# Down-products of the experts as seven quarter products, their weight sums on GpSimd, and half-row scatters

## The reference, cut to what matters

```python
def expert_choice_ffn(h, w_router, w1, w3, w2):
    n_tok, d = h.shape[1], h.shape[2]
    cap = EC_FACTOR * n_tok // N_EXPERTS
    aff = jax.nn.softmax(jnp.einsum('bnd,de->bne', h, w_router).astype(jnp.float32), axis=-1)
    gate, idx = lax.top_k(jnp.swapaxes(aff, 1, 2), cap)
    xs = jax.vmap(lambda hb, ib: hb[ib])(h, idx)
    a = jnp.einsum('becd,edf->becf', xs, w1)
    b = jnp.einsum('becd,edf->becf', xs, w3)
    y = jnp.einsum('becf,efd->becd', jax.nn.silu(a) * b, w2) * gate[..., None].astype(h.dtype)

    def combine(yb, ib):
        return jnp.zeros((n_tok, d), h.dtype).at[ib.reshape(-1)].add(yb.reshape(-1, d))

    return jax.vmap(combine)(y, idx)
...
        x_lat = x_lat + m_lat[5] * expert_choice_ffn(h_lat, router_w[layer], ...)
        if need_ctx:
            x_ctx = x_ctx + m_ctx[5] * expert_choice_ffn(h_ctx, router_w[layer], ...)
```

## Time and profile before

| | us |
|---|---|
| median of three runs | 4462.08 (4459.23 to 4466.95) |
| profiled execution, its own time | 4467.19 |
| its span, first to last instruction | 4465.3 |
| mean granted TensorE clock | 0.965 of full |

### The profile page before, as it was taken

One profiled execution on the slowest core, in us unless ns is written; L12 is line 12 of the kernel. 1 busy time (PEld: TensorE's weight loads), 2 busy tenths in 40 slices (PEclk: granted clock), 3 DMA queues, 4 the chain that ended last, 5 costly groups with the idle time before them and its releaser, 6 DMA issues. The chain is left out here.

```text
span 4465.3 us, 68193 instructions
## 1 busy us (share of the span) xinstructions
PE 4116.9 (92%) x27024; PEld 2569.5 (58%) x27024; DVE 2364.5 (53%) x4884; ACT 1132.7 (25%) x2569; POOL 229.9 (5%) x281
## 2 busy tenths in 40 slices
PE   7996899999999999996999999989999995999997
PEld 4443755888667788664444444458757773333332
DVE  6408334433576544746555555534435646666664
ACT  2011222212575322822200001031135532000001
POOL 0000000000121000000001000000000000000000
PEclk8998999999999999997999999999999996999998
DMA  7658221122421212116667767641161114888986
GB/s 280 250 90 341 70 86 39 65 106 95 156 101 67 74 58 99 33 49 254 244 251 268 280 261 281 266 155 35 51 214 32 21 58 166 322 340 327 344 332 224
DMA packets 133590, 757.35 MB, mean 170 GB/s; under 512 B 14336, under 2 KB 52992, under 8 KB 97904
## 3 DMA queue, kind: packets, MB, share of 16 engines
q1 hardware_dynamic: 108048, 670.05, 40.0%
q0 software_dynamic: 20272, 64.76, 5.4%
q10 hardware_dynamic: 5040, 19.37, 1.2%
HBM read 663.46 MB, written 91.19 MB: 169 GB/s over the span
## 5 line engine op out<-in xcount | busy, mean ns | idle before, releaser
L440 PE MATMUL psum<-w_ring,arena 128*128 128x256 f32 (+1 forms) x2784 | 611.1, 378 | 19.6 <-PEq L199 8.5
L440 PEld LDWEIGHTS psum<-w_ring,arena 128*128 128x128 f32 x2784 | 522.9, 192 | 91.3 <-issue 21.1
L3358 PE MATMUL psum<-arena 128*64 128x512 f32 x2048 | 452.5, 593 | 2.6
L3388 PE MATMUL psum<-arena 128*128 128x512 f32 x1024 | 447.9, 595 | 3.6 <-DVE arena L3655 0.9
L440 PE MATMUL psum<-arena,w_ring 128*128 128x256 f32 x1600 | 354.6, 381 | 6.4 <-DVE arena L495 3.5
L3358 PE MATMUL psum<-w_ring,arena 128*64 128x512 f32 x1536 | 343.8, 597 | 2.8 <-issue 2.8
L440 PEld LDWEIGHTS psum<-arena,w_ring 128*128 128x128 f32 x1600 | 302.9, 191 | 50.1 <-DVE w_ring L536 3.6
L3388 PEld LDWEIGHTS psum<-arena 128*128 128x128 f32 x1024 | 191.9, 190 | 237.4 <-issue 231.2
L3358 PEld LDWEIGHTS psum<-arena 128*64 128x64 f32 x2048 | 151.2, 137 | 272.7 <-issue 270.6
L3506 ACT ACTIVATE arena<-psum 128x512 f32<-128x512 f32 x128 | 76.6, 598 | 911.9 <-PE psum L3358 911.9
L1851 PE MATMUL psum<-arena 48*128 48x512 f32 (+5 forms) x1440 | 291.0, 514 | 8.9 <-PEq L1464 3.5
(11 more groups left out here) (429 smaller groups left out, 5397.8 us busy)
## 6 DMA issues: line engine op xcount, KB each, us to landing
w_ring<-in_wstream SPq DMA_DIRECT2D x162, 2048.0 KB, 9.5
arena<-in_wstream SPq DMA_DIRECT2D x97, 2048.0 KB, 7.8
x_rows<-arena SPq DMA_DIRECT2D x26, 512.0 KB, 2.7
w_ring<-in_wstream ACTq DMA_DIRECT2D x6, 2048.0 KB, 7.7
arena<-x_rows SPq DMA_DIRECT2D x18, 512.0 KB, 7.3
xn_rows<-arena POOLq DMA_DIRECT2D x18, 512.0 KB, 7.2
arena<-f_rows SPq DMA_DIRECT2D x8, 1024.0 KB, 7.3
arena<-x_rows SPq DMA_DIRECT2D x8, 1024.0 KB, 9.4
```

The source lines that it names most:

```text
L440: last = self.cr.nc.tensor.matmul(out, l, r, start=(start and k == 0), stop=(k == len(pairs) - 1), skip_group_check=True)
L3358: last = nc.tensor.matmul(cr.bank[bank][HT * h:HT * (h + 1), :], left[:, k], right[:, 4 * h + k, :], start=(start and k == 0), stop=(k == ...
L3388: last = nc.tensor.matmul(cr.bank[YB[h]][:, :], hid[:, k], W[4 + h][:, k, :], start=(k == 4), stop=(k == 3))
```

## The change

The down-product of each expert, in both layers, is made by the same scheme as the up-products. `hid` is four blocks (r, c), w2 is four blocks: D11 and D21 are tile 4, D12 and D22 tile 5. The host lays w2 out so that a tile holds both a left and a right 256-column piece of each half of the contraction (`lay_out`).

- TensorE: `down(e)` is seven `quarter`s, M1, M2, M6, M5, M7, M3, M4, each 8 matmuls of 64 output rows by 256 columns (L3447 of the new code). The two column halves of a result land on partitions 0 to 63 and 64 to 127 of one bank. In layer 0 `ctx_hidden` stands before `product_7` and `ctx_down` behind it.
- GpSimd: four sums of 128x2048 per expert, V1 = D12 - D11, V2 = D22 - V1, V3 (in D12's place) = D22 - D12, V4 = D21 - V2. V1 has a buffer of its own, V2 and V4 use T1's. V2 waits for `sum_4`, V1 for tiles 4 and 5. In layer 0 V3 waits for `ctx_down`.
- VectorE: `hidden_sums` (four of 256 elements), `out_sums` (four additions from PSUM), `out_top` and `out_bottom`; `sum_1` now also waits for the whole down-product before it (`dn`).
- ScalarE: `keep_y`, three copies out of the down-product's bank.
- The scatter is two indirect DMAs, one for each token half: `yr[r]` is [128, 512], a token's left half row on partition t, its right half on 64 + t, and the row index is doubled (`ix2`). The scatter of expert e - 1 is issued in expert e's turn, before its V sums. At the entry of each layer eight small matmuls and two VectorE instructions make the doubled lists; VectorE waits for them before `sum_0(0)` (layer 1) and `place(0)`.
- SyncE: tile 4 is free after M2, V1 and V4, tile 5 after M3, V2 and V3; its loop is unrolled. The up-products count in one semaphore (`up`) instead of seven.

```diff
+    D11, D21, D12, D22 = W[4][:, 0:4], W[4][:, 4:8], W[5][:, 0:4], W[5][:, 4:8]
+    V2, V4 = T1[:, 0:4], T1[:, 4:8]
...
+    M1B, M2B, M5B, M3B = YB[0], YB[1], HB[0], HB[1]
+    P1, P2, P6, P5, P3, P7, P4 = range(1, 8)
+    M1, M2, M6, M5, M7, M3, M4 = range(1, 8)
+    V_1, V_2, V_4, V_3 = (1, 2, 3, 4) if ctx else (1, 3, 4, 2)
...
+                if j >= 4 and ctx:
+                    sp.wait_ge(k_r, e + 1)
+                if j == 4:
+                    sp.wait_ge(dn, 7 * e + M2)
+                    sp.wait_ge(w2s, 4 * e + V_1)
+                    sp.wait_ge(w2s, 4 * e + V_4)
+                if j == 5:
+                    sp.wait_ge(dn, 7 * e + M3)
+                    sp.wait_ge(w2s, 4 * e + V_2)
+                    sp.wait_ge(w2s, 4 * e + V_3)
...
+            def sum_w1(e):
+
+                loaded(pool, 4, e)
+                loaded(pool, 5, e)
+                if e:
+                    pool.wait_ge(dn, 7 * (e - 1) + M5)
+                elif ctx:
+                    pool.wait_ge(cx_r, 4)
+                nc.gpsimd.tensor_tensor(V1, D12, D11, ALU.subtract).then_inc(w2s, 1)
+
+            def sum_w3(e):
+
+                pool.wait_ge(w2s, 4 * e + V_1)
+                if ctx:
+                    pool.wait_ge(k_r, e + 1)
+                nc.gpsimd.tensor_tensor(D12, D22, D12, ALU.subtract).then_inc(w2s, 1)
+
+            def sums_w2_w4(e):
+
+                pool.wait_ge(t_4, e + 1)
+                pool.wait_ge(w2s, 4 * e + V_1)
+                nc.gpsimd.tensor_tensor(V2, D22, V1, ALU.subtract).then_inc(w2s, 1)
+                pool.wait_ge(w2s, 4 * e + V_2)
+                nc.gpsimd.tensor_tensor(V4, D21, V2, ALU.subtract).then_inc(w2s, 1)
+
+            def scatter(e):
+
+                if e == 0:
+                    pool.wait_ge(dup_ok, 4)
+                for r in range(2):
+                    pool.wait_ge(c_e, 2 * e + r + 1)
+                    if e and r == 0:
+                        pool.wait_ge(sc, SC * e)
+                    pool.indirect_dma_start(out=x_h[:, :], out_offset=bass.IndirectOffsetOnAxis(ap=ix2[:, NE * r + e:NE * r + e + 1], axis=0),
+                                            in_=yr[r].rearrange("p c n -> p (c n)"), in_offset=None, compute_op=ALU.add).then_inc(sc, 16)
+
...
-                pool.wait_ge(c_e, 2 * e + 2)
                 if e:
-                    pool.wait_ge(sc, SC * e)
-                pool.indirect_dma_start(out=x_d[:, :], out_offset=bass.IndirectOffsetOnAxis(ap=ix[:, e:e + 1], axis=0),
-                                        in_=yr, in_offset=None, compute_op=ALU.add).then_inc(sc, 16)
+                    scatter(e - 1)
+                sum_w1(e)
                 if ctx:
-                    pool.wait_ge(k_e, e + 1)
-                    pool.indirect_dma_start(out=x_q[:, :], out_offset=bass.IndirectOffsetOnAxis(ap=ixs[:, e:e + 1], axis=0),
-                                            in_=yc, in_offset=None, compute_op=ALU.add).then_inc(sc, 16)
+                    sums_w2_w4(e)
+                    sum_w3(e)
+                    scatter_ctx(e)
+                else:
+                    sum_w3(e)
+                    sums_w2_w4(e)
+            scatter(NE - 1)
...
-                if ctx and g == 0 and some(e):
-                    pe.wait_ge(k_e, e)
+                if g == 0 and some(e):
+                    pe.wait_ge(c_e, 2 * e)
...
-                    pe.wait_ge(ug_ok, e + 1)
+                    pe.wait_ge(k_e, e + 1)
...
+            def quarter(bank, left, right, start):
+
+                for k in range(4):
+                    for h in range(2):
+                        last = nc.tensor.matmul(cr.bank[bank][HT * h:HT * (h + 1), 0:QW], left[:, k], right[:, k, QW * h:QW * (h + 1)],
+                                                start=(start and k == 0), stop=(k == 3), skip_group_check=True)
+                last.then_inc(dn, 1)
+
+            def down(e):
+
+                loaded(pe, 4, e)
                 if some(e):
-                    pe.wait_ge(c_e, 2 * e + (h - 1))
-                if h == 0:
-                    pe.wait_ge(h_ok, 4 * e + 3)
-                if ctx:
-                    pe.wait_ge(v_ok, e + 1)
-                for k in (4, 5, 6, 7, 0, 1, 2, 3):
-                    if h == 0 and k == 0:
-                        pe.wait_ge(h_ok, 4 * e + 4)
-                    last = nc.tensor.matmul(cr.bank[YB[h]][:, :], hid[:, k], W[4 + h][:, k, :], start=(k == 4), stop=(k == 3))
-                last.then_inc(c_r, 1)
+                    pe.wait_ge(c_e, 2 * e)
+                pe.wait_ge(h_ok, 4 * e + 1)
+                quarter(M1B, h_block(0, 0), D11, True)
+                pe.wait_ge(h_ok, 4 * e + 2)
+                quarter(M2B, h_block(0, 1), D21, True)
+                pe.wait_ge(hs, 4 * e + 3)
+                pe.wait_ge(w2s, 4 * e + V_2)
+                pe.wait_ge(yk, 3 * e + 1)
+                quarter(M1B, HS[1], V2, False)
+                pe.wait_ge(w2s, 4 * e + V_1)
+                quarter(M5B, HS[0], V1, True)
+                pe.wait_ge(w2s, 4 * e + V_3)
+                pe.wait_ge(yk, 3 * e + 2)
+                quarter(M1B, HS[2], D12, False)
+                loaded(pe, 5, e)
+                pe.wait_ge(hs, 4 * e + 4)
+                quarter(M3B, HS[3], D22, True)
+                pe.wait_ge(w2s, 4 * e + V_4)
+                pe.wait_ge(yk, 3 * e + 3)
+                quarter(M1B, h_block(1, 1), V4, False)
...
                 turn_hidden(e, 1)
-                ctx_hidden(e)
                 product_4(e)
                 turn_hidden(e, 2)
                 if with_x:
                     turn(e + 1)
                 turn_hidden(e, 3)
-                down(e, 0)
-                down(e, 1)
-                ctx_down(e)
+                down(e)
...
+            for r in range(2):
+                for h in range(2):
+                    for n, v in enumerate((ixf, gt)):
+                        at = 2 * NE * n + NE * r
+                        last = nc.tensor.matmul(cr.bank[M1B][HT * h:HT * (h + 1), at:at + NE], cr.const(C_ID)[:, HT * r:HT * (r + 1)], v, start=True, stop=True,
+                                                skip_group_check=True)
+            last.then_inc(dup, 1)
...
+            def keep_y(e, product, r, c):
+
+                act.wait_ge(dn, 7 * e + product)
+                if product == M1 and some(e):
+                    act.wait_ge(sc, SC * e)
+                nc.scalar.activation(yr[r][:, c], cr.bank[M1B][:, 0:QW], ACT.Copy).then_inc(yk, 1)
...
                 if some(e):
-                    dve.wait_ge(p6, e)
+                    dve.wait_ge(up, 7 * e + (P6 - 7))
+                    dve.wait_ge(dn, 7 * e)
                 tt(T1, B22, T0, ALU.subtract).then_inc(t_1, 1)
...
+            def hidden_sums(e):
+
+                dve.wait_ge(h_ok, 4 * e + 4)
+                tt(HS[0], h_block(1, 0), h_block(1, 1), ALU.add).then_inc(hs, 1)
+                tt(HS[2], h_block(0, 0), h_block(1, 0), ALU.subtract).then_inc(hs, 1)
+                dve.wait_ge(hs, 4 * e + 1)
+                tt(HS[1], HS[0], h_block(0, 0), ALU.subtract).then_inc(hs, 1)
+                dve.wait_ge(hs, 4 * e + 3)
+                tt(HS[3], h_block(0, 1), HS[1], ALU.subtract).then_inc(hs, 1)
+
+            def out_sums(e):
+
+                dve.wait_ge(yk, 3 * e + 1)
+                dve.wait_ge(dn, 7 * e + M2)
+                tt(yr[0][:, 0], yr[0][:, 0], cr.bank[M2B][:, 0:QW], ALU.add).then_inc(y_link, 1)
+                dve.wait_ge(yk, 3 * e + 2)
+                dve.wait_ge(dn, 7 * e + M5)
+                tt(yr[0][:, 1], yr[0][:, 1], cr.bank[M5B][:, 0:QW], ALU.add).then_inc(y_link, 1)
+                dve.wait_ge(yk, 3 * e + 3)
+                tt(yr[1][:, 1], yr[1][:, 1], cr.bank[M5B][:, 0:QW], ALU.add).then_inc(y_link, 1)
+                dve.wait_ge(y_link, 4 * e + 2)
+                dve.wait_ge(dn, 7 * e + M3)
+                tt(yr[0][:, 1], yr[0][:, 1], cr.bank[M3B][:, 0:QW], ALU.add).then_inc(y_link, 1)
+
+            def out_top(e):
+
+                dve.wait_ge(y_link, 4 * e + 4)
+                stt(yr[0], yr[0], gate_of(gt2[0], e), mrow, ALU.mult, ALU.mult).then_inc(c_e, 1)
+                stt(yr[1][:, 1], yr[1][:, 1], gate_of(gt2[1], e), mrow[:, 1], ALU.mult, ALU.mult)
+
+            def out_bottom(e):
+
+                dve.wait_ge(dn, 7 * e + M4)
+                stt(yr[1][:, 0], cr.bank[M1B][:, 0:QW], gate_of(gt2[1], e), mrow[:, 0], ALU.mult, ALU.mult).then_inc(c_e, 1)
...
                     place(e + 1)
                     row_sums(e + 1)
                     sum_0(e + 1)
-                    out(e, 0)
+                out_sums(e)
+                out_top(e)
+                if with_x:
                     sum_1(e + 1)
+                out_bottom(e)
+                if with_x:
                     sum_3(e + 1)
-                    out(e, 1)
-                else:
-                    out(e, 0)
-                    out(e, 1)
...
+            dve.wait_ge(dup, 1)
```

(6 more changed lines are left out.)

145 lines of the change are left out of this document (83 added, 62 removed).

## The result

The changed kernel takes 4536.54 us (median of 4 runs, 4530.47 to 4544.83), the kernel before 4461.03 in the same comparison: ratio 1.0168, 95% interval 1.0149 to 1.0187, so 75 us slower. The forecast was 4490, 28 us slower, range 4414 to 4543. The profiled execution has a span of 4535.3 us, 70.0 more than the earlier trace rows.

What follows compares the result with a forecast made beforehand. TensorE bounds the expert loops before; after, layer 1 waits on the SBUF path GpSimd and VectorE share. Layer 1 +45, layer 0 -22, DMA and ends +5 give +28 us on 4462.1: 4490 us, range 4414 to 4543.

Steps and rivals of the forecast that it cites:

- TensorE term: Down-product of each expert: seven quarters take 12.3 us instead of 13.9, 1.6 us less per expert, 51 us over 32.
- GpSimd's sums: Four 128x2048 subtractions per expert on GpSimd: 4.5 to 4.8 us each, taken as 4.6.
- Exclusion: GpSimd sums and VectorE sums of two SBUF operands exclude each other for whole instructions; shared load 40.7 us per expert.
- How the two share it: Layer 1's loop: period 44.8 us with turns, 42.4 with VectorE's run unbroken; middle taken, 3.0 us more per expert, +45.
- The slow clock: Gaps of 5 us on TensorE may lower its clock: 1.7 us per expert, +25, only in the upper bound.
- "turns" end: Layer 1: engines alternate; third quarter loses 5.3 us, product_6 0.5; period 44.8, 4.2 more than before.
- Layer 0: Layer 0's experts have room for the sums: -1.35 us per expert, 16 of them, -22.
- Entry of layer 1: Before layer 1's first product: sum_0 stands behind the doubling of the indices, so place(0) and that product come 4 us later.
- End: After layer 1's last down-product: +0.5 us; the last scatter of each layer between -0.5 and +1.
- Rival 1: No exclusion for two-operand sums, so all is hidden and the kernel takes 4416 us; chance 0.20.
- Rival 3: Down-product slots bound by weight loads: +1.4 us for each of 32 experts, +5, about 4512 us; chance 0.04.
- Rival 2: Exclusion, but balanced: VectorE unbroken, GpSimd at 4.5 us, layer 0 whole; about 4462 us, no change; chance 0.13.

Runs made afterwards that it cites:

- experiment 3: The changed kernel with each GpSimd sum of 2048 elements made as two of 1024: 4537.95 us, ratio 1.0167 to the kernel before.
- Experiment 6: The changed kernel with layer 0's context down-product one product earlier: 4530.16 us, ratio 1.0156 to the kernel before.

## Why the prediction was wrong, point by point

The direction was right and the time lies in the range, but the loss is 75 us where 28 were forecast. Of the 42 us between the forecast's +28 and the profile's +70, 17 are the sharing of the two engines, 16 layer 0, 6 the entry of layer 1 and 5 the end; unchanged code gave 2 back.

- **TensorE term: right.** 12.14 to 12.24 us for the seven quarters, 12.3 forecast. An expert gained 2.0 us by it in layer 1 instead of 1.6: 1.8 in the down-product, 0.2 in what stands before it.
- **GpSimd's sums: right.** 4.54 us alone, 4.6 forecast.
- **Exclusion: right, and the deciding point.** Whole instructions, for sums of two SBUF operands as for the copy in the earlier trace rows. The Trainium skill, SBUF — State Buffer, section Who interferes with whom, says so, and here the trace agrees: 4.72 us for a sum of 0.41 behind a GpSimd sum of 4.56.
- **How the two share it: the step that failed.** The prediction had two ends, 44.8 us per expert if turns are taken and 42.4 if VectorE's run is not broken, saw that the copy of the earlier trace rows spoke for turns, and took the middle, 3.0 us more per expert instead of 4.2. The measured period is 44.8 in the mean of the 15 and 45.1 in the steady part: the end itself. The doubt was that VectorE's own sums follow each other without a gap; they do so only while GpSimd has nothing queued (experiment 3).
- **The slow clock: a term put in the wrong place.** It stood in the upper bound only, with 1.7 us per expert. Measured are 1.4 to 3.0 us behind 13 of the loop's 14 gaps, mostly 1.7, at a granted clock of 0.83; behind one gap of 3.73 us there was no loss. Inside the "turns" end the wait for the third quarter was 4.5 instead of 5.3, and product_6 waited for nothing, since its turn came later too. The clock, which that end did not hold, made up for both, so that its 44.8 was met to the tenth is partly luck.
- **Layer 0: mis-sized.** -5.7 instead of -21.5 in the trace. The exclusion costs little there, as forecast (one wait of 2.73 us, in expert 0). But the period fell from 51.1 to 50.5, not to 49.8: the moved context steps had been priced at nothing. The second turn_hidden now stands right behind ctx_down and waits 0.62 us for out_ctx to empty bank 3, so turn_hidden 0 and 1 take 1.50 us (2474.88 to 2476.38), where the kernel before needed 0.86 from 2476.01, with the context transposes among them. These transposes by themselves and ctx_down cost some 0.5 more at their new places. Experiment 6 takes the wait away. That is 16 x 0.7 us; with the wait in expert 0 and the layer's end, where TensorE idles 15.9 us before the next layer instead of 13.5, it makes up what is missing. Why the end takes longer was not looked into.
- **Entry of layer 1: mis-sized.** +10 instead of +4. From the router's last transposes to product_1 it is 17.3 us instead of 13.0, which is the forecast's 4 for the doubled indices. The other 6 were missed: V1 and V3 wait only for their tiles, so at the entry they collide with the row sums, product_6 waits 4.3 us, and 48 instructions behind it take 12.2 us instead of 10.5 at the slower clock (0.86 of full in the mean, where the kernel before had 1.00).
- **End: missed.** The last expert has a gap like the others (4.54 us), and the five quarters behind it take 11.75 us at a granted clock of 0.75. So its down-product lasts 20.0 us instead of 14.0, and what stands behind it is 0.8 shorter: +5.
- **Unchanged code** moved by -4.1 and +2.3 us between the two profiled executions. Over all profiles of this case the start of layer 0's experts lies between 2109.6 and 2121.1 us, so single stretches of one profile are good to some 5 us.
- **Rivals.** Rival 1 (no exclusion, 4416) falls with the stretched sums; with the sums shrunk or moved away the kernel takes 4424 to 4427, 8 to 11 us above its figure. Rival 3 (slots bound by weight loads) falls with the 12.14 us. Rival 2 (exclusion, but balanced) needed VectorE's run unbroken, and the timeline has V4 between the first and the third hidden sum.

## What to carry to other kernels

Before giving VectorE's overflow to GpSimd, look whether its operations and VectorE's read two SBUF operands each: then for these instructions the two engines are one engine, which alternates instruction by instruction, and a short sum on the critical path pays for a whole long one each time. In that case count the long operation in front of each short one, don't average over orders, and put the long one behind the short ones by a wait, or make it on VectorE (2.3 us instead of 4.5) and give ScalarE the work that reads PSUM. And where a step is moved, ask who waits for its bank at the new place.
